# A two-model forward pass on one core: another order of work at the handovers between layers

## The reference

```python
def rmsnorm(x, w):
    xf = x.astype(jnp.float32)
    y = xf * lax.rsqrt(jnp.mean(xf * xf, axis=-1, keepdims=True) + NORM_EPS)
    return (y * w.astype(jnp.float32)).astype(x.dtype)

def swiglu(x, w_gate, w_up, w_down):
    return (jax.nn.silu(x @ w_gate) * (x @ w_up)) @ w_down
```

## Time and profile before

| | us |
|---|---|
| median of 3 runs | 2716.03 |
| lowest, highest | 2714.8, 2716.27 |
| the profiled execution | 2714.96 |
| span in its profile, first to last instruction | 2712.8 |
| mean granted clock of TensorE | 0.990 |

### The profile page before, as it was taken

How to read it: one execution, slowest core, us unless ns; L and a number is a source line. 1 busy time by engine, 2 the same in 40 slices (tenths; PEclk the granted TensorE clock), 3 DMA queues, 4 the chain that set the end, 5 groups by cost and what they waited for, 6 DMA issues and landing times.

```text
span 2712.8 us, 35093 instructions
## 1 busy us (share of the span) xinstructions
PE 2622.0 (97%) x12546; PEld 2159.3 (80%) x12546; DVE 2042.1 (75%) x2376; ACT 1681.3 (62%) x2188; POOL 155.0 (6%) x196
## 2 busy tenths in 40 slices
PE   7999899999999999999989999999999999999997
PEld 6888787888887887888767888788887878888886
DVE  4556657777766765554577875799999999999998
ACT  4446645454456765454464444678788787878786
POOL 2000000000000000003310000300000000000020
PEclk9999999999999999999999999899999999999999
DMA  8554306768744346754128884699999999999995
GB/s 291 190 171 163 109 32 241 248 223 299 261 162 158 125 130 238 269 172 138 63 84 307 314 289 148 225 378 372 367 387 362 388 357 378 372 378 373 361 390 223
DMA packets 284412, 687.42 MB, mean 253 GB/s; under 512 B 13428, under 2 KB 21904, under 8 KB 284304
## 3 DMA queue, kind: packets, MB, share of 16 engines
q1 hardware_dynamic: 266032, 618.65, 63.7%
q0 software_dynamic: 18272, 67.32, 7.0%
HBM read 670.19 MB, written 15.73 MB: 253 GB/s over the span
## 4 chain that ended last, share of the span: by engine, by line
PE 84%; DVE 8%; ACT 5%; issue 2%; DMA 0%; DVEq 0%; SPq 0%; ACTq 0%; POOL 0%
PE ps L2519 26%; PE ps L2521 25%; PE ps L2520 25%; DVE w_lo L1595 2%; PE ps L2667 2%; ACT w_hi L844 2%; PE ps L2751 1%; DVE xt L2365 1%; DVE xn L1674 1%; DVE h L1679 1%; PE ps L3137 0%; DVE act_lo L1663 0%; ACT hp L1257 0%; PE ps L3203 0%; PE ps L2726 0%
## 5 line engine op out<-in xcount | busy, mean ns | idle before, releaser
L1595 DVE TENSOR_TENSOR w_lo<-w_raw,w_hi 128x1024 fp32r<-128x1024 f32 x1158 | 1397.4, 1226 | 424.3 <-ACT w_hi L844 394.1
L844 ACT ACTIVATE w_hi<-w_raw 128x1024 fp32r<-128x1024 f32 x1158 | 1211.7, 1057 | 773.4 <-PE ps L2521 772.8
L2519 PE MATMUL ps<-w_hi,act_hi 128*128 128x512 f32 (+1 forms) x3424 | 1343.9, 392 | 39.0 <-DVE w_lo L1595 23.3
L2521 PE MATMUL ps<-w_lo,act_hi 128*128 128x512 f32 (+1 forms) x3424 | 1321.8, 386 | 0.0
L2520 PE MATMUL ps<-w_hi,act_lo 128*128 128x512 f32 (+1 forms) x3424 | 1320.4, 386 | 0.0
L2519 PEld LDWEIGHTS ps<-w_hi,act_hi 128*128 128x128 f32 x3424 | 646.8, 189 | 183.6 <-DVE w_lo L1595 36.8
L2521 PEld LDWEIGHTS ps<-w_lo,act_hi 128*128 128x128 f32 x3424 | 646.4, 189 | 131.5
L2520 PEld LDWEIGHTS ps<-w_hi,act_lo 128*128 128x128 f32 x3424 | 647.2, 189 | 123.4 <-issue 1.4
L1586 DVE SCALAR_TENSOR_TENSOR scr<-scr,small 128x1024 f32<-128x1024 f32 x98 | 125.2, 1278 | 0.0
L1002 ACT ACTIVATE act_hi<-ps 128x512 fp32r<-128x512 f32 (+1 forms) x87 | 62.5, 719 | 64.2 <-PE ps L2667 64.2
L1720 DVE TENSOR_TENSOR act_lo<-ps,act_hi 128x512 fp32r<-128x512 f32 (+1 forms) x87 | 74.0, 850 | 34.7 <-ACT act_hi L1002 34.7
(11 more groups left out here) (513 smaller groups left out, 1419.5 us busy)
## 6 DMA issues: line engine op xcount, KB each, us to landing
w_raw<-in_moe_w SPq DMA_DIRECT2D x337, 1024.0 KB, 6.8
scr<-in_ada_w POOLq DMA_DIRECT2D x48, 1024.0 KB, 6.7
w_raw<-in_ffn_w_gate SPq DMA_DIRECT2D x44, 1024.0 KB, 5.3
w_raw<-in_ffn_w_up SPq DMA_DIRECT2D x44, 1024.0 KB, 5.6
w_raw<-in_ffn_w_down SPq DMA_DIRECT2D x44, 1024.0 KB, 5.0
w_raw<-in_ff_w SPq DMA_DIRECT2D x42, 1024.0 KB, 5.5
w_raw<-in_odd_w_in SPq DMA_DIRECT2D x20, 1024.0 KB, 5.2
w_raw<-in_even_w_in SPq DMA_DIRECT2D x14, 1024.0 KB, 5.2
```

Source lines behind the costliest of these rows:

```text
L844: act.activation(w_hi[:, g % SPLITS, 0:c * width], w_raw[:, s % RING, o:o + c * width], ACT.Copy).then_inc(hi_done, 1)
L1595: dve.tensor_tensor(w_lo[:, g % SPLITS, 0:c * width], w_raw[:, s % RING, o:o + c * width], w_hi[:, g % SPLITS, 0:c * width].bitcast(F32), ...
L2519: pe.matmul(out_ap, hi, whi, start=start, stop=False)
L2521: return pe.matmul(out_ap, hi, wlo, start=False, stop=stop)
```

## The change

Three things change.

- In `add_post`, DVE multiplies the first half of y by factor and the norm weights as soon as the sum of squares has been read (`act_sum`), ahead of the reciprocal, and adds each half to h, scaled by the reciprocal, before it multiplies the second. This holds for all six handovers.
- In `boundary`, the parts of G+2 and the second split of block 0 come ahead of block 1's sum of squares on ACT, and the parts of G+1, G+2, G+3 and that split ahead of block 1's sums into h on DVE.
- In `lead`, of each granule the four matmuls with act_hi come first and wait for ACT's split alone, then the two with act_lo. Block 1's transposes stand behind all four granules of block 0, but for the start, where they stay behind two.

```diff
                 hi(2)
                 h_split(0, 0, col, 6)
+                hi(1)
+                h_split(0, 1, col, late)
                 post_sums(1)
-                h_split(0, 1, col, late)
-                hi(2)
+                hi(1)
                 h_split(1, 0, col, 6)
...
             def add_post(tb, factor):
 
-                dve.wait_ge(bt_done, n(bt_done))
-                link(dve.reciprocal(rstd[:, tb:tb + 1], rt[:, tb:tb + 1]))
+                dve.wait_ge(act_sum, n(act_sum))
                 for k in range(2):
                     cols = slice(k * BANK, (k + 1) * BANK)
-                    dve.scalar_tensor_tensor(xn[:, tb, cols], ps[:, 2 * tb + k, :], rstd[:, tb:tb + 1], wbc[:, cols],
+                    dve.scalar_tensor_tensor(xn[:, tb, cols], ps[:, 2 * tb + k, :], factor, wbc[:, cols],
                                              ALU.mult, ALU.mult).then_inc(dve_link, 1)
-                for k in range(2):
-                    cols = slice(k * BANK, (k + 1) * BANK)
-                    dve.wait_ge(dve_link, n(dve_link))
-                    dve.scalar_tensor_tensor(h[:, tb, cols], xn[:, tb, cols], factor, h[:, tb, cols],
+                    n(dve_link)
+                    if k == 0:
+                        dve.wait_ge(bt_done, n(bt_done))
+                        link(dve.reciprocal(rstd[:, tb:tb + 1], rt[:, tb:tb + 1]))
+                    else:
+                        dve.wait_ge(dve_link, n.last(dve_link))
+                    dve.scalar_tensor_tensor(h[:, tb, cols], xn[:, tb, cols], rstd[:, tb:tb + 1], h[:, tb, cols],
                                              ALU.mult, ALU.add).then_inc(hh_done, 1)
...
                 add_post(0, factor)
                 lo(1)
                 h_split(0, 0, col, 6)
+                lo(2)
+                h_split(0, 1, col, late)
                 lo(1)
                 add_post(1, factor)
-                h_split(0, 1, col, late)
-                lo(2)
                 h_split(1, 0, col, 6)
...
                         pe.wait_ge(lo_done, g + 1)
+                        pe.wait_ge(nhi_done, n(nhi_done))
+                        out_ap, cols = ps[:, bank + tb, 0:width], slice(tb * P, tb * P + P)
+                        for i in range(c):
+                            high, o = act_hi[:, 2 * k + i, cols], i * width
+                            pe.matmul(out_ap, high, w_hi[:, g % SPLITS, o:o + width], start=k == 0 and i == 0, stop=False)
+                            pe.matmul(out_ap, high, w_lo[:, g % SPLITS, o:o + width], start=False, stop=False)
                         pe.wait_ge(nlo_done, n(nlo_done))
                         for i in range(c):
-                            ins = three(ps[:, bank + tb, 0:width], 2 * k + i, slice(tb * P, tb * P + P), g, i * width, width,
-                                        k == 0 and i == 0, k == 3 and i == 1)
+                            o = i * width
+                            ins = pe.matmul(out_ap, act_lo[:, 2 * k + i, cols], w_hi[:, g % SPLITS, o:o + width], start=False,
+                                            stop=k == 3 and i == 1)
                         if tb:
                             ins.then_inc(gran_used, 1)
-                        if tb == 0 and k == 1:
+                        if tb == 0 and k == (1 if first else 3):
                             h_transposes(1, 0, 6, first)
                             h_transposes(1, 1, 2, first)
```

More of the change, by code:

```diff
@@ L1668, in add_post @@
             def add_post(tb, factor):
[L1670 to L1671 removed]
+                dve.wait_ge(act_sum, n(act_sum))
                 for k in range(2):
                     cols = slice(k * BANK, (k + 1) * BANK)
[L1674 removed]
+                    dve.scalar_tensor_tensor(xn[:, tb, cols], ps[:, 2 * tb + k, :], factor, wbc[:, cols],
                                              ALU.mult, ALU.mult).then_inc(dve_link, 1)
[L1676 to L1679 removed]
+                    n(dve_link)
[5 more added lines that the diff above has]
+                    dve.scalar_tensor_tensor(h[:, tb, cols], xn[:, tb, cols], rstd[:, tb:tb + 1], h[:, tb, cols],
                                              ALU.mult, ALU.add).then_inc(hh_done, 1)
             def next_rstd():
+                n(act_sum)
                 dve.wait_ge(bt_done, n(bt_done))
```

## The result

| | before | after |
|---|---|---|
| median of 7 runs, us | 2716.27 | 2725.84 |
| lowest, highest | 2713.15, 2717.67 | 2723.73, 2727.07 |
| the profiled execution, us | 2714.96 | 2723.73 |
| its span, us | 2712.8 | 2721.8 |
| its mean granted clock | 0.990 | 0.988 |

The change makes the kernel 0.38% slower: the ratio is 1.0038, with a 95% interval of 1.0029 to 1.0048. The prediction was 2719.4 with a range up to 2725; the median lies 6.4 us above the one and 0.8 above the other.

A forecast was written before the change was run, and what follows sets the result against it. PE, busy 97% of the span, was taken as the bound. Handovers +7.0, start -1.9, first handover's clock -1.6 and sixth handover -0.1 gave +3.4 us; with the profile-to-median difference 1.07, 2719.4 us, range 2714 to 2725.

The forecast's parts named there:

- What bounds the kernel: Whole kernel: PE is busy 97% of the span, so a change pays only through PE's idle time and clock.
- the chain to G+4: Five handovers: ACT and DVE work before the first matmul behind the lead (granule G+4) makes it 1.4 us later, +7.0 total.
- The table load: ACT's Silu load before the first matmul behind the lead: 1.28 us, nothing more; rival of as long again, 6.4 more, chance 0.02.
- The dependent steps on DVE: Sums into h: an instruction waiting for the one ahead starts 0.04 us after its end, costing 0.12 per dependent step.
- The halves: Sums into h by halves, norm weights multiplied before the root: block 0 gains nothing on PE, block 1 0.12 us longer.
- The start: First layer's lead, high parts first: PE begins at 13.61, 1.6 us earlier; gain 1.5 to 2.4, taken -1.9.
- The clock: First handover: its lower clock cost 1.60 us and goes away, taken -1.6, bounds -1.6 and +1.6.
- the signs that the prediction names as right: Five handovers: about 2 us idle before the first matmul behind the lead, 22.3 us stretches; first handover without lower clock.
- the forecast's own case: Whole kernel: the predicted sum holds, with its own range 2716 to 2722.5 us; chance 0.64.
- idle before G+4 lowers the clock: Rival, changed handovers: three idle stretches near 4 us lower the clock in one or two; middle 2723, chance 0.22.

The follow-up runs named there:

- after_again: The changed kernel itself, nothing altered, run again with a second profile on another group's chip; ratio 1.0042 to the kernel before.
- after_ahead: Changed kernel with the parts of the first two granules behind the lead made ahead of the next norm's squares, table load and reciprocal; ratio 0.9993 to the kernel before.
- before_look: The kernel before, nothing altered, run once more for a second profile; 2711.75 us.

## Why the prediction was wrong, step by step

**What bounds the kernel, and the chain to G+4: right.** Measured against the second handover of before: block 1's Square at +7.48 (I had 7.47), h of block 1 at +14.02 (14.0), the last four copies at +14.77 (14.75), the squares of h at +15.79 (15.75), the high part of G+4 at +19.74 (19.83), G+4 on PE at +22.16 (22.3). The idle stretch ended by DVE's w_lo is 1.94 (some 2.1). The term came out at +6.4 for five handovers where I had +7.0, inside its own 6.0 to 8.0. The last step was 3.95 instead of the 4.08 of the earlier trace rows, 0.04 of it in the squares (1.07 each instead of 1.11). The other 0.09 is that G+4's high part now waits for nothing and starts 0.09 ahead of the placeholder's end, 421.87 + 0.20 = 422.07; I had counted to that end.

**The table load: right.** Between the root of ACT and the load 0.01 to 0.02 us pass, and 0.01 between the load and what follows (420.57 + 1.28 = 421.85, and the next at 421.87). The drain that the Trainium skill states, "ScalarE: Activation LUTs", section "What ACT_TABLE_LOAD costs", has no room in these rows.

**The dependent steps on DVE: right.** Each of the new order's steps that waits for the one ahead starts 0.03 to 0.04 behind its end, where free ones start 0.08 before it: h at 415.51 after a multiply that ends at 414.79 + 0.68 = 415.47. The Trainium skill's statement in "VectorE: DVE Perf Modes", section "The DRAIN you can't avoid", that the semaphore costs nothing extra would have put block 1's h at +13.8; it came at +14.02. These are instructions of 512 columns; the page's example is another operation.

**The halves: right in the sum, wrong in the reason.** I wrote that their worth was nil. In the kernel before it is nil for PE's work (20.85 instead of 20.89), and in the changed one it is 0.3 us a handover. My chain held that 0.3 already, since I let the last four copies start apart from the first four; I had not asked what the handover would be without it.

**The start: right in kind, over-sized.** The first matmul came 1.5 us earlier over fourteen profiles (I had 1.6), and G+4 1.4, where I took 1.9 and had 1.5 as the lower bound. The compared pair showed 2.97; the G+4 of the earlier trace rows at 31.18 is the latest of all. That the pair's sum was low by 1.6 on this account was luck.

**The clock: the step that failed.** The prediction says of the first handover: "In the changed order the longest such stretches are 1.6 and 2.1. Taken: it goes, -1.6; bounds -1.6 and +1.6 (another falls)." It did go from there, and three others came, in places where before has none: +1.80, +1.65 and +1.84 in the three stages behind the third to fifth handover, and +1.92 in the first mixer. The sum is 6.4 - 2.97 - 1.60 - 0.07 + 7.3 - 0.1 = +9.0; so the term taken at -1.6 came out at about -1.60 + 7.2 = +5.6. The means of many runs on one chip say the same with less chance in it: the chain 5 x 1.27 = 6.4, the start -1.4, and after_again's 10.5 us more at the lower clock, up to 5.2, make +10.2, of +11.1 measured. All the signs that the prediction names as right were met, the clock of 1.00 in the first handover among them; they looked into the handovers, and three of the falls came 1.0 to 1.5 us behind their ends. Three errors lie in that step:

- I read the 1.60 as a property of the first handover, from one execution. It was a draw: 4 of 20 handovers in that order have it. Averaged over executions before holds about 5 x 0.2 x 1.6 = 1.6 us of such falls inside its handovers, so I had the right amount in the wrong sense, as certain in one place and impossible in the others.
- I compared stretches without a large matmul, and thought a stretch of 3.2 cut into 1.6 and 2.1 harmless. About 2 us of plain idle time with full work ahead and behind brought the clock down in 8 of 15 handovers.
- I counted one further fall as the worst of the forecast's own case, and a second as the rival's. The rival *idle before G+4 lowers the clock* had the right mechanism and a chance of 0.22; its price was made for one or two falls. With the chance of a half that the runs now show, five places make 2.5 falls, and 7.0 - 1.9 + 2.5 x 1.7 = +9.35 would have been its middle, over 0.2% by itself.

What the runs leave open: why a place falls in one execution and not in the next, and how much the first mixer has to do with the change. In the order of before the stretches at the lower clock in it add up to 13.6 to 17.1 us, in the kernels with the move 10.2 to 20.5. The spread of the kernel before over three chips, 2711.6 to 2718.5, goes with it: of its 76 runs those with a mean clock of 0.988 take 2718.1 in the mean, with 0.989 2716.9, with 0.990 2713.6 and with 0.991 2712.9.

## What to carry to other kernels

Where TensorE is the bound, price an idle stretch twice: its length, and the chance that it lowers the clock times what a fall costs (here 1.7 us, about as much as the stretch itself). Both can be told apart cheaply, by matmuls of constants into a bank that nobody reads: if the time falls while the next real matmul starts no earlier, it was the clock. And before a chain is moved back behind something useful, look for what hangs at its end: here two weight parts taken ahead of the norm's squares and the table load turned a loss of 0.4% into no loss, and with the idle time filled into a gain of 0.34%.

## What was not expected of the hardware

- A place where the clock falls in one execution and not in the next makes even large differences between two profiles worthless for a single place: the first handover took 22.49, 20.89, 20.83, 22.51 and 22.38 us in five profiles of kernels whose order there differs by nothing or by 0.06 us of work.
- A fall taken away in one place can come up in another. after_ahead has none in its handovers and, in its profile, 10.2 us more at the lower clock later than before_look's: 3.4 in each mixer and 3.4 behind a wait of 1.57 us that in before's order is followed by none.
- DVE's scalar_tensor_tensor of 128x512 takes 0.68 us with an immediate factor and 0.75 with a factor per partition. The change swaps the two forms and leaves their sum alone: before 0.75 for xn and 0.68 for h, after 0.68 and 0.75, as in the rows of DVE above.
